# A mixture of experts and the mixer behind it: an input load, a constant load, the row stores and a hold on the weight queue are moved

## What is computed

```python
for e in range(32):                       # top 2 of 32 experts for each of 256 tokens
    a = jax.nn.silu(hf @ w_e_gate[e]) * (hf @ w_e_up[e])
    out = out + gates[:, e:e + 1] * (a @ w_e_down[e])
x = rmsnorm(x + out, g_final)             # end of the first block
h = rms_norm(x, ev_norm); z = h @ ev_w_in # even mixer: pooling, latent attention with rope
m = rms_norm(mem, norm_mem); k, v = split(m @ w_kv)   # memory attention, layer 0
```

## Time and profile before

| | us |
|---|---|
| median of 3 runs | 1675.37 (1675.02 to 1677.21) |
| the profiled execution: its own time | 1676.23 |
| its span in the trace | 1674.6 |
| PE busy | 1626.1 (97%) |
| DVE busy | 1325.7 (79%) |
| ACT busy | 1035.5 (62%) |
| POOL busy | 81.1 (5%) |

### The profile page before, as it was taken

How to read it: one execution, slowest core, us unless ns; L and a number is a source line. 1 busy time by engine, 2 the same in 40 slices (tenths; PEclk the granted TensorE clock), 3 DMA queues, 4 the chain that set the end, 5 groups by cost and what they waited for, 6 DMA issues and landing times.

```text
span 1674.6 us, 27905 instructions
## 1 busy us (share of the span) xinstructions
PE 1626.1 (97%) x10552; PEld 1426.8 (85%) x10552; DVE 1325.7 (79%) x1514; ACT 1035.5 (62%) x1153; POOL 81.1 (5%) x94
## 2 busy tenths in 40 slices
PE   7999999999999999999998989999999999999998
PEld 7999999888887677777767978999999999998887
DVE  6577878855799999999986897687767879687776
ACT  5355765645789999999986464454344394453443
POOL 0000000000000000000006210000000020000000
PEclk9999999999999999999998999999999999999999
DMA  9643344366899999999998434446554565445650
GB/s 323 209 140 102 102 151 130 134 252 214 302 415 418 422 422 423 422 422 423 422 412 282 145 126 137 140 152 221 180 188 153 162 201 177 128 163 177 199 175 25
DMA packets 186667, 393.24 MB, mean 235 GB/s; under 512 B 6992, under 2 KB 151120, under 8 KB 162000
## 3 DMA queue, kind: packets, MB, share of 16 engines
q1 hardware_dynamic: 181600, 374.32, 61.1%
q0 software_dynamic: 4976, 17.67, 2.8%
HBM read 381.34 MB, written 10.62 MB: 234 GB/s over the span
## 4 chain that ended last, share of the span: by engine, by line
PE 65%; DVE 14%; DMA 10%; ACT 5%; issue 5%; POOL 0%; SPq 0%; DVEq 0%; ACTq 0%; POOLq 0%
PE ps L956 9%; DMA raw<-w_e_up_dram 8%; DVE wlo L2411 7%; PE ps L1142 6%; PE ps L962 5%; PE ps L669 4%; PE ps L674 4%; PE ps L670 4%; PE ps L971 4%; PE ps L1091 3%; PE ps L1097 3%; PE ps L1093 2%; ACT whi L1686 2%; PE ps L687 1%; PE ps L688 1%
## 5 line engine op out<-in xcount | busy, mean ns | idle before, releaser
L2411 DVE TENSOR_TENSOR wlo<-raw,whi 128x2048 fp32r<-128x2048 f32 (+2 forms) x358 | 810.5, 2278 | 138.3 <-ACT whi L1686 131.2
L1686 ACT ACTIVATE whi<-raw 128x2048 fp32r<-128x2048 f32 (+2 forms) x358 | 675.3, 1890 | 298.1 <-PE ps L962 113.7
L1091 PE MATMUL ps<-whi,xh 128*128 128x512 f32 x528 | 160.3, 396 | 0.0
L956 PE MATMUL ps<-xb,whi 128*128 128x512 f32 x672 | 160.2, 391 | 0.0
L669 PE MATMUL ps<-xh,whi 128*128 128x256 f32 x608 | 151.7, 289 | 4.6 <-DVE arena L2493 2.6
L670 PE MATMUL ps<-xl,whi 128*128 128x256 f32 x608 | 149.0, 285 | 0.0
L956 PEld LDWEIGHTS ps<-xb,whi 128*128 128x128 f32 x672 | 124.1, 188 | 24.3
L1097 PE MATMUL ps<-wlo,xh 128*128 128x512 f32 x528 | 143.3, 396 | 1.4 <-DVE wlo L2411 1.4
L669 PEld LDWEIGHTS ps<-xh,whi 128*128 128x128 f32 x608 | 117.7, 194 | 6.0 <-DVE arena L2493 3.0
L1097 PEld LDWEIGHTS ps<-wlo,xh 128*128 128x128 f32 x528 | 97.2, 188 | 29.5 <-DVE wlo L2411 9.6
L670 PEld LDWEIGHTS ps<-xl,whi 128*128 128x128 f32 x608 | 117.9, 194 | 0.3
(11 more groups left out here) (509 smaller groups left out, 3184.5 us busy)
## 6 DMA issues: line engine op xcount, KB each, us to landing
raw<-w_e_gate_dram SPq DMA_DIRECT2D x64, 1024.0 KB, 10.1
raw<-w_e_up_dram SPq DMA_DIRECT2D x64, 1024.0 KB, 10.3
raw<-w_e_down_dram SPq DMA_DIRECT2D x64, 1024.0 KB, 10.3
raw<-ffn_w_gate_up_dram SPq DMA_DIRECT2D x44, 1024.0 KB, 5.1
raw<-w_in_dram SPq DMA_DIRECT2D x30, 1024.0 KB, 5.9
raw<-ffn_w_down_dram SPq DMA_DIRECT2D x22, 1024.0 KB, 4.9
raw<-xa_w_kv_dram SPq DMA_DIRECT2D x16, 1024.0 KB, 5.5
raw<-xa_w_q_dram SPq DMA_DIRECT2D x8, 1024.0 KB, 5.1
```

The costliest lines, as they stand in the source:

```text
L956: nc.tensor.matmul(ps[:, bank + b, :], wh[:, k, b * P:b * P + P], xb[:, k, :, :].rearrange("p a t -> p (a t)"), start=k == 0, stop=False, ...
L1091: nc.tensor.matmul(o, h[:, k, :], wh[:, k, :], start=part == 0 and k == 0, stop=False)
L1686: nc.scalar.activation(whi[u % HL][:, 0:n], raw[u % RAW][:, 0:n], ACT.Copy).then_inc(hi_ready, 1)
L2411: v.tensor_tensor(wlo[u % HL][:, 0:n], raw[u % RAW][:, 0:n], whi[u % HL][:, 0:n].bitcast(F32), ALU.subtract).then_inc(lo_ready, 1)
```

## The change

Four things change, all around the end of the experts. The memory tokens for layer 0 go to another place in the arena (`mem_first`, chunks 44 to 51) and POOL loads them, and the positions, right behind the store of tile 3. The constants `c2` are loaded behind the four gathers, once DVE has summed the squares of the memory tokens, and the positions are converted after that. A store moves no more rows than its tile can have: 512 / (m + 1), rounded down, less 128 for a second pass, and at most 128; POOL's store loops are written out. SP waits for all four gathers to land ahead of the load of the mixer's first unit `u_ev[0]`.

```diff
-        mem = chunks(0, 8)
+        mem, mem_first = chunks(0, 8), chunks(44 * T, 8)
...
-        posi, posf = area(23 * T, T), area(53 * T, T)
+        posf = area(53 * T, T)
...
                 else:
+                    if u == u_ev[0]:
+                        for a in range(4):
+                            sp.wait_ge(y_landed[a], 16)
                     load(u, units[u][0])
                     u += 1
...
-            def rows_of(m):
+            def rows_of(m, part):
 
-                return P if m < HEAVY else SLOTS if m < FEW else SLOTS // 2
+                return min(P, PAIRS_OUT // (m + 1) - part * P)
...
             pool.wait_ge(starts_there, 1)
-            for m in range(HEAVY):
-                for s in passes(m):
-                    store(s, P)
-            for first, end in ((HEAVY, FEW), (FEW, TILES - 3)):
-                assert (end - first) % LOOP == 0
-                with pool.Fori(0, (end - first) // LOOP) as i:
-                    for m in range(first, first + LOOP):
-                        store(passes(m)[0], rows_of(m), i)
-            pool.wait_ge(win_h, PASSES - 2)
-            pool.wait_ge(win_l, PASSES - 2)
-            pool.dma_start(mem, kview(t["memT"])).then_inc(mem_landed, 16)
-            store(PASSES - 3, rows_of(TILES - 3))
-            pool.wait_ge(mem_landed, 32)
-            pool.dma_start(c2, t["const2"]).then_inc(second_landed, 16)
-            pool.dma_start(posi.bitcast(I32), t["positions_2"].partition_broadcast(P)).then_inc(second_landed, 16)
-            store(PASSES - 2, rows_of(TILES - 2))
-            pool.wait_ge(second_landed, 32)
-            link(g.tensor_copy(posf, posi.bitcast(I32)))
-            store(PASSES - 1, rows_of(TILES - 1))
+            for m in range(TILES):
+                for part, s in enumerate(passes(m)):
+                    store(s, rows_of(m, part))
+                if m == TWICE:
+                    pool.wait_ge(gath_mm, 16)
+                    pool.dma_start(mem_first, kview(t["memT"])).then_inc(mem_landed, 16)
+                    pool.dma_start(posf.bitcast(I32), t["positions_2"].partition_broadcast(P)).then_inc(second_landed, 16)
             pool.wait_ge(y_stored, 16 * PASSES)
             for tt in range(2):
                 for k in range(2):
                     pool.indirect_dma_start(y_back[:, 2 * tt + k, :], None, compact[0:PAIRS_OUT, :], ...)
+            pool.wait_ge(mem_squared, 1)
+            pool.dma_start(c2, t["const2"]).then_inc(second_landed, 16)
+            pool.wait_ge(second_landed, 32)
+            link(g.tensor_copy(posf, posf.bitcast(I32)))
```

More of the change, by code:

```diff
@@ L1966, in mem_high @@
                     for c in (2 * a, 2 * a + 1):
-                        last = nc.scalar.activation(xh[:, c, :], mem[:, c, :], ACT.Copy, scale=vcol("xa_m0", c))
+                        last = nc.scalar.activation(xh[:, c, :], mem_first[:, c, :], ACT.Copy, scale=vcol("xa_m0", c))
                     last.then_inc(xh_ready, 1)
@@ L2149, in _ @@
             for b in range(2):
-                last = nc.scalar.activation(mem_sq[:, 4 * b:4 * b + 4, :], mem[:, 4 * b:4 * b + 4, :], ACT.Square)
+                last = nc.scalar.activation(mem_sq[:, 4 * b:4 * b + 4, :], mem_first[:, 4 * b:4 * b + 4, :], ACT.Square)
             last.then_inc(mem_sq_there, 1)
@@ L2777, in mem_low @@
                     for c in (2 * a, 2 * a + 1):
-                        last = v.scalar_tensor_tensor(out=xl[:, c, :], in0=mem[:, c, :], scalar=vcol("xa_m0", c),
+                        last = v.scalar_tensor_tensor(out=xl[:, c, :], in0=mem_first[:, c, :], scalar=vcol("xa_m0", c),
                                                       in1=xh[:, c, :].bitcast(F32), op0=ALU.mult, op1=ALU.subtract)
@@ L3464, in _, with row_start, store @@
             g.tensor_copy(xc_l[:, :, PAIRS_OUT:], wide_zeros).then_inc(tails_set, 1)
-            def row_start(s, i=None):
-                at = start_i[0:1, s:s + 1] if i is None else start_i[0:1, bass.ds(i * LOOP + s, 1)]
-                return pool.value_load(at, min_val=0, max_val=PAIRS_OUT)
-            def rows_of(m):
-                return P if m < HEAVY else SLOTS if m < FEW else SLOTS // 2
-            def store(s, n, i=None):
-                row = row_start(s, i)
-                pool.wait_ge(r_y, (0 if i is None else i * LOOP) + s + 1)
+            def row_start(s):
+                return pool.value_load(start_i[0:1, s:s + 1], min_val=0, max_val=PAIRS_OUT)
+            def rows_of(m, part):
+                return min(P, PAIRS_OUT // (m + 1) - part * P)
+            def store(s, n):
+                row = row_start(s)
+                pool.wait_ge(r_y, s + 1)
                 pool.sem_inc(store_go, 1)
-                if i is not None or s >= 1:
-                    pool.wait_ge(y_stored, (0 if i is None else i * (16 * LOOP)) + 16 * s)
+                if s >= 1:
+                    pool.wait_ge(y_stored, 16 * s)
                     pool.sem_inc(store_go, 1)
```

## The result

The changed kernel takes **1678.8 us** in the median of 10 runs (1677.88 to 1680.98) where the kernel before, on the same chip, takes 1675.19 (1671.26 to 1679.36). The ratio is 1.0018, with a 95% interval of 1.001 to 1.0026: some 3 us slower. The forecast was 0.8 us faster. The profiled execution took 1678.84 us, its span is 1677.1.

What follows compares the result with a forecast made beforehand. DMA transfers bound the expert stage, another chain its end. 2.5 us faster in the experts, less 1.2 for the hold and 0.5 for the constants, gave 0.8 faster: 1674.5 us against the median 1675.37, range 1669.5 to 1680.5.

Steps and rivals of the forecast that it cites:

- the gain of 2.6 us at the end of the experts: Last expert tile: down-unit conversions come 2.6 us sooner without the memory load beside them, so the last store gains 2.6 us.
- Memory tokens at tile 3: Behind the store of tile 3: tokens cost 2.6 us, less 0.7 of idle room, plus 0.3 for positions.
- the idle capacity of 0.7 us: DMA engines from 456 to 530 us: idle room taken as 0.7 us, between 0.4 and 1.1.
- the sign: Expert stage: the chain runs over a weight transfer earlier, near 500 to 515 us, not 532.
- Rows: Smaller stores in tiles 4 to 28: 1.7 us less, up to 3.8; second store of tile 2: 0.4 less.
- whole rows in equal lots: Tiles 4 to 28: rows split over 16 DMA engines, rounded up, 73 instead of 84: 1.7 us less, light tiles nothing.
- the even sum: Tiles 4 to 28: rows spread evenly over the 16 DMA engines, 59.4 for each: 3.8 us less.
- The hold: Expert end to mixer start: gathers gain 7 us, held unit's load spends it, transposes 1.2 us slower, later mixer units free.
- The constants: Angle sequence behind the gathers: ends near 926 or 929 us, hidden by some 4 us; 0.5 us charged, 0 to 1.5.
- Quick gathers: Gathers before the mixer: issue in 0.94 us each even beside DVE, 3.1 us faster, whole 1670.2; chance 0.25.
- Stores on few engines: Expert stores from tile 4: rows on as many engines as divide them, 5.0 us slower, whole 1681.2; chance 0.15.
- the hold in full: Mixer start: gathers landed at 904.5, slow first load, angles late: 3.6 + 1.5 us slower, whole 1677.9; chance 0.15.

Runs made afterwards that it cites:

- rows by 16: The changed kernel with every store's rows rounded up to a multiple of 16: 1679.38 us, ratio 1.0022.
- the smaller stores alone: The kernel before with only the stores' row limits changed; memory tokens, constants and SP's wait as before: 1673.73 us, ratio 0.9985.
- the scale-first run: The changed kernel, with ACT scaling the second half's rows before it converts the held unit: 1676.63 us, ratio 1.0008.
- the hold at the third unit: The changed kernel with SP's wait moved from ahead of u_ev[0] to ahead of u_ev[2]: 1677.01 us, ratio 0.9997.
- the constants early: The kernel before with smaller stores, constants and positions loaded behind tile 0, memory tokens at their old place, SP's wait ahead of u_ev[2]: 1671.32 us, ratio 0.9963.
- the hold alone: The kernel before with only SP's wait for the gathers ahead of u_ev[0] added: 1680.12 us, ratio 1.002.
- light tiles of 16 rows: The kernel before with the smaller stores, and only 16 rows stored in tiles 15 to 31: 1672.27 us, ratio 0.9978.
- the old loads once more: The changed kernel with SP's wait ahead of u_ev[2], tokens and positions behind tile 0, plus the old loads repeated into unread arena: 1676.68 us, ratio 1.0005.

## Why the prediction was wrong

The sum said 2.5 us faster in the experts, 1.2 slower by the hold, 0.5 by the constants. Measured in the same places: 0.35 slower, and 2.4 slower for the two together. The remaining 0.5 in the stretch to the end and 0.7 the other way ahead of the first store (390.36, before 391.09) are no larger than what these stretches move by themselves. With the 2.5 us of the experts, added on paper, the change would have come out level; without them it is slower.

**The step that failed is the gain of 2.6 us at the end of the experts**, "which is what the load beside them costs; behind the second a chain of computing runs to the last store". Of these 2.6 us none is left (33.51 against 33.17). The step has three faults. It read tile 30's units as the last tile's. It took the whole delay of a conversion for a delay of PE: with the loads gone PE is done with tile 30 only 1.1 us sooner behind tile 28's store, and 0.9 to 1.6 sooner in all eight kernels that lack the old loads (20.50 to 21.21 us, against 22.07). And it took the computing behind it to be as long as before, while PE does it in part at 1.2 GHz: tile 31's six groups take 7.12 us instead of 5.54. With rows by 16, where the clock stays up, 1.6 us are left. My rivals had no such case; that a clock can fall behind a pause of PE was not asked of any step.

**Memory tokens at tile 3.** 2.2 us was the price; it is 2.75 (3.1 against the kernel with the smaller stores alone). That is the price of the bytes, 2.9, in full, so the idle capacity of 0.7 us hardly helped. Why not is open; the clock at 504 us is not the reason. That the chain enters a weight transfer earlier was right, by the name of the sign, and too timid (500 to 515 us; it is 487.76).

**Rows.** 2.1 us with tile 2, measured 3.1, inside the two ends (1.7 and 3.8, and 0 to 0.8 for tile 2). That the light tiles gain nothing held. The choice of whole rows in equal lots was right there only. By tile 15 it allows 2.1 to 2.5 us, the even sum 3.4 (354 rows at 0.155 for 16), and 3.3 came. It is luck that the two sizes nearly cancel, about 3 gained by rows and 3 lost by the tokens, so that the stretch to tile 28 is the same to 0.01 us.

**The hold.** The mechanism came as told: gathers landed at 903.6 (903.0 forecast), the unit at 909.3 (908.4), an idle stretch of 9.8 us on ACT (7 to 9), the scale behind the conversion, transposes at 913.64 (912.9). The forecast left the last store at its old time and took 1.2 us, and it came out 1.9 us behind before at the transposes. In the seam the two terms are 2.4 where I had 1.7. That the other mixer units "cost nothing" fell with the scale-first run: the split of x stands behind them as well.

**The constants.** "It stays hidden by some 4 us" was right for the changed kernel, with the sequence's end at 927.6 where I had 926 to 929, some 7 us ahead of the norm (934.78). It was true only because of the hold. Without it they cost 3.6 us, and with the hold at the third unit about as much (a seam of 44.01 us, 40.36 with the constants early). Adding prices that hide each other was a weakness of the working, though not what turned the sign.

**The rivals.** Quick gathers is out: one gather of four took 0.94 us, the others 1.80, 1.98 and 2.96. The reason that I gave for long issues is not whole either, since the quick one (895.06) ran beside DVE instructions with two SBUF inputs. Stores on few engines is out too. In the changed kernel the profile's time from issue to landing is 8.1 us for 102 rows, 7.2 for 85 and 6.7 for 73, where the rule wanted over 11.3 for the last; before, 128 rows took 8.4 to 9.2 and 64 rows 6.3 to 7.7. The time from issue to landing of the stores of tiles 4, 5 and 6, one row each:

```profile
DMA to landing us min/median/max: 8.1/8.1/8.1
...
DMA to landing us min/median/max: 7.2/7.2/7.2
...
DMA to landing us min/median/max: 6.7/6.7/6.7
```

Of the two readings in the Trainium skill, page "DMA: Bandwidth & Descriptors", section on why a DMA increments its semaphore by 16, it is the exception, rows divided by 16 and rounded up, that these landings and the light tiles bear out. The heavier tiles came nearer to the even sum, which this reading alone doesn't give. The third rival, the hold in full, gave the nearest time (1677.9) by the wrong sum: it kept a gain in the experts.

**What stays open** is why the clock falls at 878 us. Each kernel has one profile, so it isn't known whether it falls in every execution. The kernel before, the smaller stores alone, the hold alone, rows by 16 and light tiles of 16 rows kept 1.00 there; the changed kernel and the other eight dropped to about 0.5, with the same pause of 1.43 us ahead. The old transfers in flight don't keep it up (the old loads once more), nor does the memory load at its old place (the constants early). PE's waits ahead of the pause don't decide it either: the constants early have one of 1.33 us ahead of tile 30's groups and a fall, rows by 16 have none there and no fall. What the order of the rows before the pause has to do with it wasn't settled.

## What to carry to other kernels

A transfer that is moved has two prices, and both want the stage's limit: what it frees at the old place is worth only as much as the work behind it then does not slow down or wait elsewhere, and what it takes at the new one is paid in full once the queues are flat. Follow a transfer to the engine that ends the stage: here a conversion that comes 2.2 us sooner gave PE 1.1. Ahead of a hold on a weight queue, read what each engine has in its order behind the first held unit; here the same hold two units later made the seam 3.4 us shorter. And where two delays lie under one another, take each out alone before calling one of them hidden: the constants looked free only beneath the hold.

## What was not expected of the hardware

- The granted clock halved behind a pause of PE of 1.43 us in some kernels and stayed at 1.00 in others with the same pause; it cost 1.6 us, six matmul groups in 7.12 against 5.54 and 5.55, at the end of the experts.
- A gather's issue on POOL took 0.94 us in the quickest case, and up to 4.20 while DVE was busy in the kernel with the hold alone. The four together took from 7.3 us (old loads once more, 894.42 to 901.72) to 11.0 (rows by 16, 891.88 to 902.88), for one and the same work.
- The 785 KB of constants took 6.3 us from issue to their use under the hold and 9.5 with weight loads beside them.
